# Hybrid NSA, pooling and HGRN2 block: four HGRN decay levels joined into two products of 192 queries, evictions moved from VectorE to ScalarE, and the compression slabs placed four later

## The chip, the cores and the metric

One core of a Trainium2 chip runs the kernel. The metric is the device time of one execution in microseconds (us). In what follows, PE is TensorE (matrix products), DVE is VectorE, ACT is ScalarE, POOL is GpSimd, and SP is the engine that issues the transfers.

## What is computed

One layer over 256 tokens of width 1024, in float32. The normalised input is multiplied by one wide matrix `w_in`, and the columns feed three mixers: sparse attention with compressed, selected and windowed keys, causal pooling, and HGRN2, a gated linear recurrence. Each mixer's output is gated, projected, merged and sent through `w_out`. The change lies in HGRN2, whose reference is, per chunk:

```
A = jnp.cumsum(lf, axis=2)
o_inter = jnp.einsum('bhtd,bhde->bhte', qq * jnp.exp(A), S)
rel = jnp.where(tri[:, :, None], A[:, :, :, None, :] - A[:, :, None, :, :], -jnp.inf)
att = jnp.einsum('bhtd,bhsd,bhtsd->bhts', qq, kk, jnp.exp(rel))
o_intra = jnp.einsum('bhts,bhse->bhte', att, vv)
```

`lf` is the logarithm of the forget gate. The score of query t and key s is a sum over 128 channels of q·k·exp(A[t] − A[s]). The exponent depends on both, and the kernel splits it at an edge e that lies between s and t: exp(A[t] − A[e]) goes into the query and exp(A[e] − A[s]) into the key, so that a plain matrix product gives the score and neither factor can overflow.

## The kernel before

**Slabs.** Every large product is cut into slabs of 256 output columns. `plan_slabs` lists 67 of them, numbered from 0, and every engine walks that list in order. Slabs 0 to 3 are the forget gates (`f`), 4 to 11 are HGRN queries and values in turn (`hq`, `hv`), 12 and 13 the keys and values of the compression (`kc`, `vc`), 14 and 15 attention values (`vs`, `vw`), 16 the attention gates (`gate`, 48 columns), 17 a query slab (`q`), 18 to 21 the pooling input (`bv`), and then the rest. A slab's weights land in `W` by a transfer. ACT rounds them to a high part `WH` (`hi`, L420), DVE subtracts that from `W` for a low part `WL` (`lo`, L603), and PE multiplies three pairs of parts into one PSUM bank: 48 matmuls at L970, 24 for `gate`. Two PSUM banks alternate, so `read(s)` on ACT or DVE must have emptied the bank of slab s before the product of slab s + 2 begins. `WL` has two buffers, so `lo(s)` waits for the end of product s − 2.

**HGRN between the slabs.** There are 8 heads of 256 tokens, and a unit u is one head's half of 128 tokens: 16 units, numbered 0 to 15. With `U0 = 9`, PE issues in slab 9 + u, ahead of that slab's product, `hg_scores(u)` and then `hg_values(u - 1)`. Before the change a unit's scores are five products of 64 queries (edges at multiples of 64, 32, 16, 8 and 4 tokens, L995), one of 128 queries for blocks of 4 tokens (L996) and, for the second half of a head, one across the halves (L999). Values are L1011 and L1013. At slabs 14, 18, 22 and 26 PE adds a sum of squares for the head norm (L1041).

What prepares a unit, in the order of the chain:

- DVE, at slabs 2, 6, 10 and 14: `scan` (L624), the running sum A of two heads (a pair).
- POOL: 12 subtractions for a pair (L348, L350, L352). Pairs 2 and 3 also wait until the scores of 4(p − 1) units are done, since the tiles are used again: pair 3 waits for unit 7, in slab 16.
- ACT, at slabs 6, 10, 14 and 18: exponentials of the pair (L433 to L439).
- DVE, at slab 7 + 2h: the multiplications of head h (L648 to L652), 14 instructions. `hg_scores` of the head waits for them (`s_hmul`).
- DVE, at slab s, `early(s)`: the masks of unit s − 9. It copies each product's valid part into `PM` (L708, L709, L716). Each is chained to the one before it. `hg_values(u)` waits for them (`s_hmask`).
- DVE, at slabs 11 + 2h, copies head h's result out of PSUM (L636), and ACT squares it (L443). At slabs 14, 18, 22 and 26 ACT turns the sums of squares into a factor with two table loads (L450, L451), and DVE multiplies two heads by it (`norm`, L639, waits `s_hrs`).

For slabs 9 to 24 the order of DVE within slab s is: `early(s)`, `lo(s + 1)`, the scan, norm and head multiplications that fall on s, and `read(s)`. The order of ACT is: exponentials, squares and norm factor of s, `read(s)`, `hi(s + 3)`. Every engine executes its list in order.

Of the kernel before, what the change touches and what calls it, by code (L numbers as in the profile page):

```python
# [26 lines left out]
LEVELS = (128, 64, 32, 16, 8, 4)  # L27
NLV = len(LEVELS)
SMALL_K, SMALL_Q = NLV, NLV + 1

# [7 lines left out]
K_MASK, K_ID, K_ONE = 0, 448, 576  # L38
K_BLOCK = K_MASK + 64 * (NLV - 1)
K_CMASK, K_VALID, K_COUNT = 704, 734, 736  # L40
K_ROWS, K_ALL = 800, 804
# [32 lines left out]
BY_ACT = ("f", "gate", "bv", "q", "ks", "kw", "silu", "merge", "out")  # L74
BY_DVE = ("hq", "hv", "kc", "vc", "ks", "kw", "vs", "vw", "q", "silu", "branch", "out")
# [13 lines left out]
def trunk(nc, x, small, consts, w_in, cmp_w, pool_w, w_branch, w_out, post_norm, out):  # L89
# [14 lines left out]
    with ctx:  # L104
# [42 lines left out]
        QK = [R[:, 4 + 2 * b:6 + 2 * b, :].rearrange("p a (l h t) -> p (a l) h t", h=2, t=T) for b in range(2)]  # L147
# [174 lines left out]
        def _(pool):  # L322
# [12 lines left out]
            for p in range(4):  # L335
# [7 lines left out]
                for i, b in enumerate(LEVELS):  # L343
                    n = 2 * T // (2 * b)
                    av = a2.rearrange("p (n w) -> p n w", w=2 * b)
                    dv = QK[p % 2][:, i].rearrange("p h t -> p (h t)").rearrange("p (n w) -> p n w", w=2 * b)
                    edge = av[:, :, b - 1:b].to_broadcast((P, n, b))
                    last = pool.tensor_tensor(dv[:, :, 0:b], edge, av[:, :, 0:b], ALU.subtract)  # L348
                    if i:
                        pool.tensor_tensor(dv[:, :, b:2 * b], av[:, :, b:2 * b], edge, ALU.subtract)  # L350
                mid = RHO[:, p].rearrange("p (n a) -> p n a", a=1).to_broadcast((P, 2 * T // 4, 4))
                pool.tensor_tensor(QK[p % 2][:, SMALL_K].rearrange("p h (n w) -> p (h n) w", w=4),  # L352
# [54 lines left out]
        def _(act):  # L407
# [14 lines left out]
            def mix(s):  # L422
# [5 lines left out]
                for p in range(4):  # L428
                    if s == U0 - 3 + 4 * p:
                        act.wait_ge(s_sub, p + 1)  # L430
                        act.wait_ge(s_scan, p + 1)
                        q = QK[p % 2]
                        act.activation(q[:, 0, :, P:T], HA[:, 2 * p:2 * p + 2, P:T], ACT.Exp)  # L433
                        act.activation(q[:, 0, :, 0:P], q[:, 0, :, 0:P], ACT.Exp)
                        act.activation(q[:, 1:NLV].rearrange("p l h t -> p (l h t)"),
                                       q[:, 1:NLV].rearrange("p l h t -> p (l h t)"), ACT.Exp)
                        small = q[:, SMALL_K].rearrange("p h t -> p (h t)")
                        act.activation(q[:, SMALL_Q].rearrange("p h t -> p (h t)"), small, ACT.Exp)
# [69 lines left out]
            def read(s):  # L508
# [4 lines left out]
                if kind == "f":  # L513
# [76 lines left out]
        def _(dve):  # L590
# [27 lines left out]
            def mix(s):  # L618
# [14 lines left out]
                for h in range(HG):  # L633
                    if s == U0 + 2 + 2 * h:
                        dve.wait_ge(s_hpv, 2 * h + 2)
                        dve.tensor_copy(OC[:, h, :], ps[:, 6, 0:T]).then_inc(s_hoc, 1)  # L636
                    if s == U0 + 5 + 4 * (h // 2):
                        dve.wait_ge(s_hrs, h // 2 + 1)
                        dve.scalar_tensor_tensor(out=OC[:, h, :], in0=OC[:, h, :], scalar=st_hn[:, h:h + 1], in1=RS[:, h % 2],  # L639
                                                 op0=ALU.mult, op1=ALU.mult).then_inc(s_hn, 1)  # L640
                for h in range(HG):
                    if s == U0 - 2 + 2 * h:
                        dve.wait_ge(s_hexp, h // 2 + 1)
                        for i, b in enumerate(LEVELS):
                            ev = QK[h // 2 % 2][:, i, h % 2].rearrange("p (n w) -> p n w", w=2 * b)
# [4 lines left out]
                        sk, sq_ = QK[h // 2 % 2][:, SMALL_K, h % 2], QK[h // 2 % 2][:, SMALL_Q, h % 2]  # L650
# [134 lines left out]
            def read(s):  # L785
# [458 lines left out]
```

## Time and profile before

| | |
|---|---|
| time, median of 3 runs | 491.25 us (491.23 to 491.64) |
| the profiled execution | 491.25 us, of which the span is 489.4 us |
| busy PE, DVE, ACT, POOL | 474.8, 359.8, 255.9, 157.4 us |
| PE clock granted | 0.999 of 2.4 GHz over the span |
| share of the chain that ended last | PE 88%, DVE 9% |

The span runs from the first to the last instruction. A busy time is a sum over an engine's instructions as the profiler models them. What an instruction costs in a dense row is the distance between the starts of two neighbours, which for PE is shorter than the printed duration, since matmuls overlap.

### The profile page before, as it was taken

The page shows a single profiled execution, that of the slowest core. Times are in us where ns is not written, and L with a number is a line of the kernel's source. Part 1 is how long each engine was busy: PE and PEld are TensorE (multiplying, and loading weights), DVE is VectorE, ACT ScalarE, POOL GpSimd, SP SyncE. Part 2 cuts the span into 40 slices and gives each one's busy share as a digit, 9 for nine tenths or more (in the row PEclk, how much of TensorE's full clock was granted, in tenths as well). Part 3 has the DMA queues.
Part 4 walks back from the last instruction along what each step waited for, and adds up shares of the span by engine and source line. Part 5 has one row for each costly group of instructions (what it writes and reads, how often), then busy time and mean ns, then how long its engine had stood idle before and what let it go on. Part 6 is the DMA issues. An engine that isn't in the chain of part 4 may idle for free.

```text
span 489.4 us, 9629 instructions
## 1 busy us (share of the span) xinstructions
PE 474.8 (97%) x3938; PEld 462.8 (95%) x3938; DVE 359.8 (74%) x647; ACT 255.9 (52%) x379; POOL 157.4 (32%) x157
## 2 busy tenths in 40 slices
PE   3999999999999999999999999999999999999995
PEld 3999999999899999999999999999999999999995
DVE  4897999899978775989696755888674357655653
ACT  6966635363484555844366444566554245433541
POOL 1072800702800006992067334546645220000000
PEclk9999999999999999999999999999999999999999
DMA  9965553325525485355537235234435535767502
GB/s 298 322 193 176 173 173 93 98 86 173 173 88 172 137 209 173 97 173 174 171 107 239 87 90 168 88 102 158 130 129 173 174 95 192 232 218 255 173 1 86
DMA packets 77030, 76.43 MB, mean 156 GB/s; under 512 B 6783, under 2 KB 75775, under 8 KB 76987
## 3 DMA queue, kind: packets, MB, share of 16 engines
q1 hardware_dynamic: 76699, 75.64, 49.5%
q8 instruction: 31, 0.51, 0.4%
q10 hardware_dynamic: 288, 0.18, 0.2%
q14 instruction: 12, 0.10, 0.1%
HBM read 74.77 MB, written 1.05 MB: 155 GB/s over the span
## 4 chain that ended last, share of the span: by engine, by line
PE 88%; DVE 9%; DMA 1%; issue 1%; ACT 0%; DVEq 0%
PE ps L970 71%; PE ps L1142 3%; DVE WL L603 3%; PE ps L995 2%; PE ps L1094 2%; PE ps L1083 1%; PE ps L1158 1%; DVE R L648 1%; DVE CP L813 1%; DVE R L649 1%; PE ps L1110 1%; DMA R<-x 1%; DVE PM L716 1%; PE ps L1097 1%; PE ps L1112 1%
## 5 line engine op out<-in xcount | busy, mean ns | idle before, releaser
L970 PE MATMUL ps<-hH,WL 128*128 128x256 f32 x696 | 200.6, 288 | 1.0 <-DVE WL L603 1.0
L970 PE MATMUL ps<-hL,WH 128*128 128x256 f32 x696 | 197.7, 284 | 0.0
L970 PE MATMUL ps<-hH,WH 128*128 128x256 f32 x696 | 197.7, 284 | 0.0
L603 DVE TENSOR_TENSOR WL<-W,WH 128x2048 fp32r<-128x2048 f32 x66 | 152.2, 2307 | 16.1 <-PE ps L970 15.7
L420 ACT ACTIVATE WH<-W 128x2048 fp32r<-128x2048 f32 x66 | 124.6, 1889 | 58.4 <-PE ps L970 58.3
L970 PEld LDWEIGHTS ps<-hH,WL 128*128 128x128 f32 x696 | 132.8, 191 | 2.2 <-DVE WL L603 1.2
L970 PEld LDWEIGHTS ps<-hL,WH 128*128 128x128 f32 x696 | 132.8, 191 | 0.8 <-issue 0.7
L970 PEld LDWEIGHTS ps<-hH,WH 128*128 128x128 f32 x696 | 132.8, 191 | 0.0
L381 POOL TENSOR_SCALAR R<-R,st 128x256 f32<-128x256 f32 x32 | 29.2, 923 | 80.1 <-DVE st L782 80.1
L970 PE MATMUL ps<-bH,WL 128*128 128x256 f32 x192 | 54.9, 286 | 0.0
L970 PE MATMUL ps<-bL,WH 128*128 128x256 f32 x192 | 54.3, 283 | 0.0
L970 PE MATMUL ps<-bH,WH 128*128 128x256 f32 x192 | 54.3, 283 | 0.0
L541 ACT ACTIVATE TG<-ps 128x512 f32<-128x512 f32 x24 | 14.4, 599 | 64.8 <-PE ps L970 64.8
L348 POOL TENSOR_TENSOR R<-R 128x256 f32<-128x256 f32 x24 | 24.1, 1011 | 74.5 <-PE ps L999 49.1
L970 PE MATMUL ps<-WL,hH 128*128 128x256 f32 x160 | 46.0, 287 | 0.9 <-DVE WL L603 0.9
L970 PE MATMUL ps<-WH,hL 128*128 128x256 f32 x160 | 45.3, 283 | 0.0
L970 PE MATMUL ps<-WH,hH 128*128 128x256 f32 x160 | 45.3, 283 | 0.0
L970 PEld LDWEIGHTS ps<-bH,WL 128*128 128x128 f32 x192 | 36.8, 192 | 0.2 <-issue 0.2
L970 PEld LDWEIGHTS ps<-bL,WH 128*128 128x128 f32 x192 | 36.8, 192 | 0.1
L970 PEld LDWEIGHTS ps<-bH,WH 128*128 128x128 f32 x192 | 36.8, 192 | 0.0
L384 POOL TENSOR_SCALAR R<-R,st 128x128 f32<-128x128 f32 x32 | 35.8, 1131 | 0.0
L970 PEld LDWEIGHTS ps<-WL,hH 128*128 128x128 f32 x160 | 30.7, 192 | 1.5 <-DVE WL L603 1.3
(191 smaller groups left out, 756.0 us busy)
## 6 DMA issues: line engine op xcount, KB each, us to landing
W<-w_in SPq DMA_DIRECT2D x49, 1024.0 KB, 5.2
W<-w_branch SPq DMA_DIRECT2D x12, 1024.0 KB, 5.0
W<-w_out SPq DMA_DIRECT2D x4, 1024.0 KB, 5.4
R<-x SPq DMA_DIRECT2D x2, 512.0 KB, 4.6
W<-w_in SPq DMA_DIRECT2D x2, 512.0 KB, 6.7
R<-cmp_w SPq DMA_DIRECT2D x2, 512.0 KB, 8.4
OC<-pool_w SPq DMA_DIRECT2D x4, 256.0 KB, 5.8
R<-x SPq DMA_DIRECT2D x1, 1024.0 KB, 7.2
```

The lines of the kernel that those rows point to most:

```text
L348: last = pool.tensor_tensor(dv[:, :, 0:b], edge, av[:, :, 0:b], ALU.subtract)
L381: pool.tensor_scalar(pp[:, 256 * j:256 * j + 256], pp[:, 256 * j:256 * j + 256], w[:, j:j + 1], None, ALU.mult)
L384: last = pool.tensor_scalar(pp[:, 512 + 128 * j:640 + 128 * j], pp[:, 512 + 128 * j:640 + 128 * j], w[:, 2 + j:3 + j], None, ALU.mult)
L420: act.activation(WH[:, s % 3, :, 0:n], W[:, s % 3, :, 0:n], ACT.Copy).then_inc(s_hi, 1)
L541: act.activation(TG[:, tslot(s), :], bank(s), ACT.Tanh, scale=0.5).then_inc(s_read_a, 1)
L603: dve.tensor_tensor(WL[:, s % 2, :, 0:n], W[:, s % 3, :, 0:n], WH[:, s % 3, :, 0:n], ALU.subtract).then_inc(s_lo, 1)
L648: dve.tensor_tensor(ev[:, :, 0:b], ev[:, :, 0:b], kv[:, :, 0:b], ALU.mult)
L649: dve.tensor_tensor(ev[:, :, b:2 * b], ev[:, :, b:2 * b], qv[:, :, b:2 * b], ALU.mult)
L970: mm = pe.matmul(o, l, r, start=(k == 0 and j == 0 and not (split and c)), stop=(k == KC - 1 and j == 2 and not (split and not c)))
L995: pe.matmul(ps[:, b0, 64 * (lv - 1):64 * lv], t, up, start=(lv == 1), stop=False)
L1094: pe.matmul(ps[:, 2, :], queries(h, 1), KS[:, part, g].rearrange("p a t -> p (a t)"), start=(part == 0), stop=(part == 1))
L1142: mm = pe.matmul(ps[64 * hh:64 * hh + 64, 6, at:T], v, p, start=(j == 0), stop=(j == count - 1))
```

## The change

The edges at 32 and 16 become one product, and so do those at 8 and 4 (`RADIX = (16, 4)`). For blocks of b tokens in groups of four, block j's queries are laid out once for every earlier block of their group: three blocks reach back one, two reach back two, one reaches back three (`STEPS`), six blocks of queries where there were four blocks of tokens. A key has one decay factor, to its own block's end (`OWN`), and the query copy carries the rest (`REACH`). The edges at 64 (`HALF`) and 128 (`TOP`) and the blocks of 4 tokens stay. `TOP` is now in another tile, `CVD`. ACT instead of DVE now reads `hq`, `hv`, `vs` and `vw` out of PSUM and copies the heads' results. `kc` and `vc` move from slabs 12 and 13 to 16 and 17, so that `vs`, `vw`, `gate` and `q` stand at 12 to 15.

```diff
-LEVELS = (128, 64, 32, 16, 8, 4)
-NLV = len(LEVELS)
-SMALL_K, SMALL_Q = NLV, NLV + 1
+RADIX = (16, 4)
+STEPS = ((0, 3, 1), (3, 2, 2), (5, 1, 3))
...
-    out += [("kc", 0, "in", C_KC), ("vc", 0, "in", C_VC), ("vs", 0, "in", C_VS), ("vw", 0, "in", C_VW),
-            ("gate", 0, "in", C_GATE), ("q", 2, "in", C_Q + 2 * SLAB)]
+    out += [("vs", 0, "in", C_VS), ("vw", 0, "in", C_VW), ("gate", 0, "in", C_GATE), ("q", 2, "in", C_Q + 2 * SLAB),
+            ("kc", 0, "in", C_KC), ("vc", 0, "in", C_VC)]
...
-BY_ACT = ("f", "gate", "bv", "q", "ks", "kw", "silu", "merge", "out")
-BY_DVE = ("hq", "hv", "kc", "vc", "ks", "kw", "vs", "vw", "q", "silu", "branch", "out")
+BY_ACT = ("f", "hq", "hv", "vs", "vw", "gate", "bv", "q", "ks", "kw", "silu", "merge", "out")
+BY_DVE = ("kc", "vc", "ks", "kw", "q", "silu", "branch", "out")
...
+        DEC = [R[:, 4 + 2 * b:6 + 2 * b, :].rearrange("p a n -> p (a n)") for b in range(2)]
+        TOP = [CVD[:, 2 * b:2 * b + 2, :] for b in range(2)]
+        HALF = [d[:, 0:512].rearrange("p (h t) -> p h t", h=2) for d in DEC]
+        OWN = [[d[:, 512 + 1280 * r:1024 + 1280 * r].rearrange("p (h t) -> p h t", h=2) for r in range(2)] for d in DEC]
+        REACH = [[d[:, 1024 + 1280 * r:1792 + 1280 * r].rearrange("p (h t) -> p h t", h=2) for r in range(2)]
+                 for d in DEC]
+        SMALL_K = [d[:, 3072:3584].rearrange("p (h t) -> p h t", h=2) for d in DEC]
+        SMALL_Q = [d[:, 3584:4096].rearrange("p (h t) -> p h t", h=2) for d in DEC]
...
+                for r, b in enumerate(RADIX):
+                    n = 2 * T // b
+                    av = a2.rearrange("p (n w) -> p n w", w=b)
+                    pool.tensor_tensor(OWN[p % 2][r].rearrange("p h (n w) -> p (h n) w", w=b),
+                                       av[:, :, b - 1:b].to_broadcast((P, n, b)), av, ALU.subtract)
+                    aw = a2.rearrange("p (n j w) -> p n j w", j=4, w=b)
+                    to = REACH[p % 2][r].rearrange("p h (n j w) -> p (h n) j w", j=6, w=b)
+                    for at, count, far in STEPS:
+                        pool.tensor_tensor(to[:, :, at:at + count], aw[:, :, far:4],
+                                           aw[:, :, 0:count, b - 1:b].to_broadcast((P, n // 4, count, b)), ALU.subtract)
                 mid = RHO[:, p].rearrange("p (n a) -> p n a", a=1).to_broadcast((P, 2 * T // 4, 4))
...
-                        act.wait_ge(s_hoc, h + 1)
-                        act.activation(SQ[:, h % 2], OC[:, h, :], ACT.Square).then_inc(s_hsq, 1)
+                        act.wait_ge(s_hpv, 2 * h + 2)
+                        act.wait_ge(s_scan, h // 2 + 1)
+                        act.activation(SQ[:, h % 2], ps[:, 6, 0:T], ACT.Square).then_inc(s_hsq, 1)
+                        act.activation(OC[:, h, :], ps[:, 6, 0:T], ACT.Copy).then_inc(s_hoc, 1)
...
+                if kind == "hq":
+                    act.activation(HQ[:, 2 * n:2 * n + 2, :], b2, ACT.Copy).then_inc(s_read_a, 1)
+                elif kind == "hv":
+                    act.activation(HV[:, :, SLAB * n:SLAB * n + SLAB], b2, ACT.Copy).then_inc(s_read_a, 1)
+                elif kind in ("vs", "vw"):
+                    act.activation(VV[:, 0 if kind == "vs" else 1], b2, ACT.Copy).then_inc(s_read_a, 1)
...
-                    if s == U0 + 2 + 2 * h:
-                        dve.wait_ge(s_hpv, 2 * h + 2)
-                        dve.tensor_copy(OC[:, h, :], ps[:, 6, 0:T]).then_inc(s_hoc, 1)
                     if s == U0 + 5 + 4 * (h // 2):
                         dve.wait_ge(s_hrs, h // 2 + 1)
+                        dve.wait_ge(s_hoc, h + 1)
...
+                        for r, b in enumerate(RADIX):
+                            dve.tensor_tensor(OWN[e][r][:, hp], OWN[e][r][:, hp], HK[:, h], ALU.mult)
+                            qv = HQ[:, h].rearrange("p (n j w) -> p n j w", j=4, w=b)
+                            ev = REACH[e][r][:, hp].rearrange("p (n j w) -> p n j w", j=6, w=b)
+                            for at, count, far in STEPS:
+                                dve.tensor_tensor(ev[:, :, at:at + count], ev[:, :, at:at + count], qv[:, :, far:4],
+                                                  ALU.mult)
...
-                    for lv in range(1, NLV):
-                        b = LEVELS[lv]
-                        r = slice(0, b if lv == 1 else P)
-                        to = PM[r, u % 2, 0:P].rearrange("p (n w) -> p n w", w=2 * b)[:, :, b:2 * b]
-                        c = slice(64 * (lv - 1), 64 * lv)
-                        last = dve.copy_predicated(to, K[r, c].bitcast(mybir.dt.uint32).rearrange(
-                            "p (n w) -> p n w", w=b), ps[r, b0, c].rearrange("p (n w) -> p n w", w=b))
-                        if lv < NLV - 1:
-                            link(last)
-                    last.then_inc(s_hmask, 1)
+                                             ps[:, b0 + 1, P:2 * P]))
+                    for r, b in enumerate(RADIX):
+                        c = slice(192 * r, 192 * r + 192)
+                        to = PM[:, u % 2, 0:P].rearrange("p (n j w) -> p n j w", j=4, w=b)
+                        on = K[:, c].bitcast(mybir.dt.uint32).rearrange("p (n j w) -> p n j w", j=6, w=b)
+                        src = ps[:, b0, c].rearrange("p (n j w) -> p n j w", j=6, w=b)
+                        for at, count, far in STEPS:
+                            link(dve.copy_predicated(to[:, :, far:4], on[:, :, at:at + count], src[:, :, at:at + count]))
+                    dve.tensor_copy(PM[0:64, u % 2, 64:P], ps[0:64, b0, 384:448]).then_inc(s_hmask, 1)
                 h = s - H0 - 2
...
-                q = QK[p % 2]
-                for lv in range(1, NLV):
-                    b = LEVELS[lv]
-                    t = q[:, lv, hp, P * i:P * i + P]
-                    up = t.rearrange("p (n w) -> p n w", w=2 * b)[:, :, b:2 * b]
-                    pe.matmul(ps[:, b0, 64 * (lv - 1):64 * lv], t, up, start=(lv == 1), stop=False)
-                mm = pe.matmul(ps[:, b0, K_BLOCK:K_BLOCK + P], q[:, SMALL_K, hp, P * i:P * i + P],
-                               q[:, SMALL_Q, hp, P * i:P * i + P], start=False, stop=True)
+                e, t = p % 2, slice(P * i, P * i + P)
+                for r in range(2):
+                    pe.matmul(ps[:, b0, 192 * r:192 * r + 192], OWN[e][r][:, hp, t],
+                              REACH[e][r][:, hp, 192 * i:192 * i + 192], start=(r == 0), stop=False)
+                pe.matmul(ps[:, b0, 384:448], HALF[e][:, hp, t], HALF[e][:, hp, P * i + 64:P * i + P],
+                          start=False, stop=True)
+                mm = pe.matmul(ps[:, b0 + 1, P:2 * P], SMALL_K[e][:, hp, t], SMALL_Q[e][:, hp, t],
+                               start=True, stop=(i == 0))
                 if i:
-                    mm = pe.matmul(ps[:, b0 + 1, 0:P], q[:, 0, hp, 0:P], q[:, 0, hp, P:T], start=True, stop=True)
+                    mm = pe.matmul(ps[:, b0 + 1, 0:P], TOP[e][:, hp, 0:P], TOP[e][:, hp, P:T], start=False, stop=True)
                 mm.then_inc(s_hp, 1)
```

**PE, the scores of an odd unit and the values of the one before it.** In the rows below `R` holds the decayed keys and queries and `K`-named operands are constants. Before:

```order
L995 MATMUL ps<-R 128x64 x5
L996 MATMUL ps<-R 128x128
L999 MATMUL ps<-R 128x128
L1011 MATMUL ps<-PM,R 128x128
```

After the change:

```order
L1013 MATMUL ps<-R 128x192 x2
L1015 MATMUL ps<-R 128x64
L1017 MATMUL ps<-R 128x128
L1020 MATMUL ps<-CVD 128x128
L1032 MATMUL ps<-PM,R 128x128
```

Five products of 64 queries become two of 192 and one of 64. What follows them stays.

**ACT, slabs 13 and 14.** Before, from the square of head 1 (L443) to the next `hi`. `WH<-W 128x8x48` is the narrow `gate` slab, L433 to L439 the exponentials of pair 2, L450 and L451 the norm factor of pair 0:

```order
L443 ACTIVATE TG<-OC 128x256
L420 ACTIVATE WH<-W 128x8x48
L433 ACTIVATE R<-R 128x2x128
L434 ACTIVATE R<-R 128x2x128
L435 ACTIVATE R<-R 128x2560
L438 ACTIVATE R<-R 128x512
L439 ACTIVATE R<-R 128x512
L450 ACT_TABLE_LOAD
L450 ACTIVATE TG<-ps,st 128x512
L451 ACT_TABLE_LOAD
L451 ACTIVATE TG<-TG 128x512
L420 ACTIVATE WH<-W 128x2048
```

After the change, from the copy of head 1's result:

```order
L458 ACTIVATE OC<-ps 128x256
L534 ACTIVATE VV<-ps 128x512
L435 ACTIVATE WH<-W 128x2048
L448 ACTIVATE CVD<-R 128x2x128
L449 ACTIVATE CVD<-CVD 128x2x128
L450 ACTIVATE R<-R 128x3072
L451 ACTIVATE R<-R 128x512
L452 ACTIVATE R<-R 128x512
L465 ACT_TABLE_LOAD
L465 ACTIVATE TG<-ps,st 128x512
L466 ACT_TABLE_LOAD
L466 ACTIVATE TG<-TG 128x512
```

The read of `vw` (L534) stands ahead of a full `hi` where a narrow one stood, and the largest exponential is 3072 wide.

**DVE, slab 15.** Before, from the narrow `lo` of slab 16 (L603): the copy of head 2, and the first six of the 14 multiplications of head 4:

```order
L603 TENSOR_TENSOR WL<-W,WH 128x8x48
L636 COPY OC<-ps 128x256
L648 TENSOR_TENSOR R<-R 128x128
L649 TENSOR_TENSOR R<-R 128x128
L648 TENSOR_TENSOR R<-R 128x2x64
L649 TENSOR_TENSOR R<-R 128x2x64
L648 TENSOR_TENSOR R<-R 128x4x32
L649 TENSOR_TENSOR R<-R 128x4x32
```

After the change, from the end of the multiplications of head 4, after which the `q` slab is read, to the read of `kc` (L836) in slab 16:

```order
L673 TENSOR_TENSOR R<-R 128x256
L677 TENSOR_TENSOR R<-R 128x16x12
L677 TENSOR_TENSOR R<-R 128x16x8
L677 TENSOR_TENSOR R<-R 128x16x4
L680 TENSOR_TENSOR R<-R 128x256
L681 TENSOR_TENSOR R<-R 128x256
L823 TENSOR_TENSOR QS<-ps,QS 64x2x256 x2
L737 COPY PM<-ps 128x128
L738 COPY_PREDICATED PM<-K,ps 128x128
```

The head's multiplications by tokens in pairs of halves become, for each radix, one over 256 keys and three over 192 queries' worth in steps of 12, 8 and 4 (or 48, 32 and 16) columns. They still number 14. The mask stage that follows has six chained copies of 96, 64 and 32 columns, twice, and a plain one of 64 instead of five of 64. The narrow `lo` moves from slab 15 to slab 13, since it belongs to `gate`.

## Rows read from the trace of the kernel before

**Rows 1.** Page: busy time of PE, and the chain that ended last.

```profile
PE 474.8 (97%) x3938; PEld 462.8 (95%) x3938; DVE 359.8 (74%) x647; ACT 255.9 (52%) x379; POOL 157.4 (32%) x157
...
PE 88%; DVE 9%; DMA 1%; issue 1%; ACT 0%; DVEq 0%
```

**Rows 2.** Waits of PE: total us, times, longest us.

```profile
PE ps L1166 <- DVE R L869: 7.4, 1, 7.4
PE ps L970 <- DVE WL L603: 1.9, 3, 1.0
```

**Rows 3.** Chain in order of time: start us, us until the next piece, what.

```profile
78.86 1.06 PE ps L995 x10
79.93 0.28 PE ps L996 x2
80.65 5.75 PE ps L970 x48
...
125.47 6.02 PE ps L970 x48
...
133.28 0.86 PE ps L1041 x2
...
268.40 1.73 PE ps L1083 x8
```

**Rows 4.** Timeline of DVE, slabs 12, 13 and 17: start us, us, instruction, shape, count.

```profile
97.36 0.30 DVE L709 COPY_PREDICATED PM<-K,ps 128x128 f32<-128x128 uint32 x1
97.69 1.27 DVE L716 COPY_PREDICATED PM<-K,ps 64x64 f32<-64x64 uint32 x5
98.87 2.29 DVE L603 TENSOR_TENSOR WL<-W,WH 128x2048 fp32r<-128x2048 f32 x1
...
101.41 0.28 DVE L648 TENSOR_TENSOR R<-R 128x128 f32<-128x128 f32 x1
...
103.83 0.43 DVE L651 TENSOR_TENSOR R<-R 128x256 f32<-128x256 f32 x1
...
104.49 3.34 DVE L813 TENSOR_TENSOR CP<-ps,V 64x240 f32<-64x240 f32 x8
...
134.67 1.39 DVE L798 TENSOR_TENSOR QS<-ps,QS 64x512 fp32r<-64x512 f32 x2
```

**Rows 5.** Timeline of DVE, slab 7, head 0.

```profile
56.04 0.70 DVE L648 TENSOR_TENSOR R<-R 128x128 f32<-128x128 f32 x1
56.66 0.73 DVE L649 TENSOR_TENSOR R<-R 128x128 f32<-128x128 f32 x1
```

**Rows 6.** Timeline of POOL, pair 1 beside rows 5, and pair 2.

```profile
56.55 0.69 POOL L350 TENSOR_TENSOR R<-R 128x256 f32<-128x256 f32 x1
...
89.84 2.66 POOL L348 TENSOR_TENSOR R<-R 128x256 f32<-128x256 f32 x1
...
93.05 0.61 POOL L348 TENSOR_TENSOR R<-R 128x256 f32<-128x256 f32 x1
...
96.68 1.11 POOL L352 TENSOR_TENSOR R<-R,BR 128x512 f32<-128x512 f32 x1
```

**Rows 7.** Timeline of ACT, slab 14, and a read of slab 18.

```profile
102.26 0.40 ACT L433 ACTIVATE R<-R 128x256 f32<-128x256 f32 x1
...
110.09 1.90 ACT L420 ACTIVATE WH<-W 128x2048 fp32r<-128x2048 f32 x1
...
142.40 0.58 ACT L520 ACTIVATE R<-ps 128x512 f32<-128x512 f32 x1
```

**Rows 8.** Timelines of DVE and POOL where pair 3 starts beside head 4.

```profile
120.06 0.42 DVE L652 TENSOR_TENSOR R<-R 128x256 f32<-128x256 f32 x1
...
119.75 1.77 POOL L348 TENSOR_TENSOR R<-R 128x256 f32<-128x256 f32 x2 [21.97 <-PE ps L999]
```

**Rows 9.** Windows after the last matmul: busy us of the engines (count), PEclk, DMA share, GB/s.

```profile
484.00:485.00 1.00, 0.17 (x2) 0.00 (x0) 0.46 (x3) 0.57 (x3) 0.00 (x0) 1.00 0.62 229
488.00:489.00 1.00, 0.00 (x0) 0.00 (x0) 0.00 (x0) 0.00 (x0) 0.00 (x0) 0.53 0.50 188
```

More of the change, by code:

```diff
@@ L35 @@
 GATES = 3 * HEADS
[L38 to L41, printed above, removed]
+K_MASK, K_BLOCK, K_ID, K_ONE = 0, 384, 512, 640
+K_CMASK, K_VALID, K_COUNT = 768, 798, 800
+K_ROWS, K_ALL = 864, 868
 K_CAUSAL = K_ALL
@@ L146, in trunk @@
         HV = R[:, 3, :].rearrange("p (i n) -> p i n", i=TT)
-        QK = [R[:, 4 + 2 * b:6 + 2 * b, :].rearrange("p a (l h t) -> p (a l) h t", h=2, t=T) for b in range(2)]
+        DEC = [R[:, 4 + 2 * b:6 + 2 * b, :].rearrange("p a n -> p (a n)") for b in range(2)]
[6 more added lines that the diff above has]
+        SMALL_Q = [d[:, 3584:4096].rearrange("p (h t) -> p h t", h=2) for d in DEC]
         xin = R[:, 4, :].rearrange("p (i n) -> p i n", i=TT)
@@ L431, in mix @@
                         act.wait_ge(s_scan, p + 1)
-                        q = QK[p % 2]
[L433 to L438, printed above, removed]
+                        top, small = TOP[p % 2], SMALL_K[p % 2].rearrange("p h t -> p (h t)")
+                        act.activation(top[:, :, P:T], HA[:, 2 * p:2 * p + 2, P:T], ACT.Exp)
+                        act.activation(top[:, :, 0:P], top[:, :, 0:P], ACT.Exp)
+                        act.activation(DEC[p % 2][:, 0:3072], DEC[p % 2][:, 0:3072], ACT.Exp)
+                        act.activation(SMALL_Q[p % 2].rearrange("p h t -> p (h t)"), small, ACT.Exp)
                         act.activation(small, small, ACT.Exp, scale=-1.0).then_inc(s_hexp, 1)
@@ L643, in mix @@
                         dve.wait_ge(s_hexp, h // 2 + 1)
-                        for i, b in enumerate(LEVELS):
-                            ev = QK[h // 2 % 2][:, i, h % 2].rearrange("p (n w) -> p n w", w=2 * b)
+                        dve.wait_ge(s_read_a, ACT_READS[WHERE[("hq", h // 2)]])
+                        e, hp = h // 2 % 2, h % 2
+                        for b, to in ((128, TOP), (64, HALF)):
+                            ev = to[e][:, hp].rearrange("p (n w) -> p n w", w=2 * b)
                             kv = HK[:, h].rearrange("p (n w) -> p n w", w=2 * b)
@@ L793, in read @@
                 b2 = b.rearrange("p (c t) -> p c t", c=2)
-                if kind == "hq":
-                    last = dve.tensor_copy(HQ[:, 2 * n:2 * n + 2, :], b2)
-                elif kind == "q":
+                if kind == "q":
                     for src, own, other in query_halves(s):
                         last = dve.tensor_tensor(other, src, own, ALU.subtract)
-                elif kind == "hv":
-                    last = dve.tensor_copy(HV[:, :, SLAB * n:SLAB * n + SLAB], b2)
                 elif kind in ("kc", "vc"):
@@ L818, in read @@
                         last = dve.tensor_tensor(other, src, hi_own, ALU.subtract)
-                elif kind in ("vs", "vw"):
-                    last = dve.tensor_copy(VV[:, 0 if kind == "vs" else 1], b2)
                 elif kind == "silu":
@@ L1004, in hg_values @@
                 pe.wait_ge(s_hmask, u + 1)
-                pe.wait_ge(s_read_v, DVE_READS[WHERE[("hv", h // 2)]])
+                pe.wait_ge(s_read_a, ACT_READS[WHERE[("hv", h // 2)]])
                 if h and i == 0:
@@ L1120, in at_values @@
                 if pair == 0:
+                    pe.wait_ge(s_read_a, ACT_READS[WHERE[("vw", 0)]])
                     pe.wait_ge(s_pct, 1)
@@ L1189, in constant_table @@
     s = np.arange(P)[:, None]
-    j = np.arange(64)[None, :]
-    for n, b in enumerate(LEVELS[1:]):
-        t = (j // b) * 2 * b + b + j % b
-        k[:, K_MASK + 64 * n:K_MASK + 64 * n + 64] = (s // (2 * b) == t // (2 * b)) & (s % (2 * b) < b)
+    j = np.arange(192)
+    for n, b in enumerate(RADIX):
+        step = j // b % 6
+        far = np.array([1, 1, 1, 2, 2, 3])[step]
+        key = 4 * (j // (6 * b)) + np.array([0, 1, 2, 0, 1, 0])[step]
+        assert (far + key % 4 < 4).all()
+        k[:, K_MASK + 192 * n:K_MASK + 192 * n + 192] = s // b == key[None, :]
     t = np.arange(P)[None, :]
```

17 lines of the change are left out of this document (8 added, 9 removed).

## Prediction, made before the changed kernel had run

> **What bounds the kernel now.** I read the busy times first: PE works in 97% of the span and is 88% of the chain that ended last [rows 1]. The table of waits then shows how little is left to win by removing waits: after its start PE idles three times, 1.9 us in all, each time for `lo` on DVE [rows 2]. The chain in order of time shows the beat of an HGRN slab: 1.79 us of scores and values (from 78.86 to 80.65), then 5.75 us of product, 7.54 us together [rows 3]. So a shorter score block is a gain only while DVE keeps up. The 9% of DVE in the chain is the warning: where `kc` and `vc` add 3.34 us each [rows 4], DVE has more work than a slab of 7.54 us has room for. I therefore went through the DVE timeline slab by slab, and through POOL's beside it.
>
> **PE.** Each float32 product is two passes. Ten passes over 64 queries take 1.06 us, 0.106 each; eight over 256 take 1.73 us, 0.216 each [rows 3]. The narrow ones stand on a floor, the wide ones cost 0.84 ns a column, so a pass over 192 should take 0.162. Eight passes (0.85) become four (0.65): 0.20 us less per unit, 3.2 us over 16 units. Bounds: four passes at the floor of 0.106 save 6.8 us in all; four at the 256-wide 0.216 save nothing. A score block is now 1.59 us; the scores of an even unit end 1.14 us into it, those of an odd one 1.36.
>
> **DVE per slab.** Masks: one of 128 columns takes 0.33 to the next start (97.36 to 97.69), and five of 64 take 1.18 to `lo` at 98.87, the last of them unchained [rows 4]. Six chained ones of 96, 64 and 32 columns average about 0.25, and the plain copy 0.2: 0.33 + 1.50 + 0.20 = 2.03 in place of 1.51, with bounds of 1.8 and 2.3. Multiplications of a head: twelve of 128 columns take 2.42 (101.41 to 103.83), 0.20 each, and those of 256 take 0.33 each (103.83 to 104.49) [rows 4]. By that slope 192 and 64 cost 0.27 and 0.13, so a head takes 4 × 0.20 + 2 × (0.33 + 0.27 + 0.20 + 0.13) + 2 × 0.33 = 3.3 in place of 3.1. Copies of `hq`, `hv`, `vs`, `vw` and the results leave DVE. On ACT each read is at most 0.58 [rows 7], and ACT is busy in 52% of the span [rows 1] with a single 1.9 us `hi` in most slabs [rows 7], so outside slab 14 they cost nothing; if that cover went, a slab would pay 0.6. No transfer changes.
>
> **POOL.** Alone it takes 0.58 for 256 columns (93.05 to the next start) and 1.11 for 512 [rows 6]; 384 and 128 lie at 0.85 and 0.32. A pair is 3 × 0.58 + 2 × (1.11 + 0.85 + 0.58 + 0.32) + 1.11 = 8.6 us, against 7.5. What matters more: when POOL and a DVE instruction with two SBUF inputs meet, one waits. At 56 us DVE's 0.20 became 0.62 (56.04 to 56.66), in step with POOL's 0.66 [rows 5, 6], and one POOL subtraction took 2.66 across a `lo` [rows 6]. The Trainium skill, "SBUF — State Buffer", SBUF: two separate sides, states it as an exclusive lock held for a whole instruction; by that rule the trace agrees, and without it the collision below would cost nothing.
>
> **The walk.** First, slab 14, with T the end of product 13. `gate` now stands here, with half a product. PE: block 1.59, squares 0.86 [rows 3], half a product 2.9, block 1.59, product 5.75, block 1.59: it wants product 16 at T + 14.3. ACT must do the read of `vw` 0.5, a full `hi` 1.8, then what took 102.26 to 110.09, 7.8, and 0.4 for 512 more columns [rows 7]: the norm factor is there at T + 10.5. DVE waits for it and does norm (two of 256, 0.8), the masks of unit 6 (2.03) and `lo(16)` (2.2 [rows 4]): T + 15.6. PE waits 1.3. Before, DVE came to the norm so late that this factor was ready.
>
> Second, slab 15, from X = T + 15.6, when product 16 starts (6.0 after a stall [rows 3]). DVE begins head 4. POOL's pair 3 has been free since the scores of unit 7, at T + 14.05, and was held by `lo(16)`; it starts at X too. They alternate, one DVE instruction for each of POOL's twelve, so head 4 lasts as long as the pair: 8.6, with 0.1 of each DVE instruction between, 9.8, and the last two multiplications, 10.4 us instead of 3.3. Behind it on DVE stand `q` 1.4 [rows 4], the masks of unit 7 with their plain copy 2.2, and `lo(17)` 2.2: X + 16.3. PE wanted product 17 at 6.0 + 1.6 = X + 7.6. It waits 8.7, of which 4.4 for the multiplications (`s_hmul`) ahead of unit 8's scores, 2.5 for the masks, 1.8 for `lo`.
>
> Third, `kc` and `vc`, from Y, the start of product 17. DVE: `kc` 3.4, masks 2.0, `lo` 2.2, head 5 3.3, `vc` 3.4, masks 2.2, `lo(19)` 2.2: Y + 18.7. PE: 6.0, block 1.59 with 0.86, 5.75, block 1.59: Y + 15.8. It waits 3.0. After that DVE has one head or none per slab and catches up; later slabs stand as before.
>
> Slab 9 has head 0 against pair 1, which grows by 1.1 us while DVE loses two reads ahead of it; I take 1.1 us for its wait of 0.5.
>
> Sum: waits 1.1 + 1.3 + 8.7 + 3.0 = 14.1 in place of 1.9; 0.25 for one more restart (6.02 against 5.75 [rows 3]); 3.2 saved. 491.25 + 14.1 − 1.9 + 0.25 − 3.2 = 500.5. The profiled execution took 491.25, the median too. The same walk through the old order gives product 17 some 2 us too late, because it lets POOL in at 119.75 where head 4 in fact ran on to 120.4 and POOL waited (1.77 for two) [rows 8]. I take 1 us off: **499.5**.
>
> **The rivals.** *The collision does not happen* (POOL is not yet asking, or yields as at 119.75). Then head 4 takes 3.3, the slab 15 wait is 9.1 − 7.6 = 1.5, and the waits sum to 0.5 + 1.3 + 1.5 + 3.0 = 6.3: 492.7. For it speaks only the one place where POOL was starting cold; here it has waited since T + 14.05.
>
> *Faster:* the reads taken from DVE let it reach head 4 before unit 7's scores release POOL, and `kc` and `vc` fall where it has slack. Then PE keeps 3.2 and loses only 0.5: 491.25 − 3.2 − 1.9 + 0.5 = 486.6. It decides at slab 14: head 4 must end by T + 14.05, so start by T + 10.7, which is 4.9 us earlier than in my walk. The wait for the norm is 2.8 of these; that and 2 us of masks and `lo` would have to go. Against it: the ACT chain is rows of before, moved by a full `hi`.
>
> *The clock falls.* The last matmul lies in the window from 484 us; the granted clock is 1.00 until 488 and 0.53 on average in the next window [rows 9]. So PE at rest for about 4 us went to 1.2 GHz, and the wait of 4.4 us in slab 17 is as long. Half a product at half speed would add 2.9: 502.4. The Trainium skill, "TensorE: Matmul & The Clock Gate", What's actually happening, says that an idle engine falls to the lower level and comes back after sustained work; by that rule, the trace agrees for the fall, and no row shows a fall in mid-kernel.
>
> *No change* needs gains and waits to cancel, between the second rival and the first.
>
> **How the numbers follow.** My case 0.58, with 495 to 503 as its own range (masks at 1.8 or 2.3 move three mask stages and with them 1.5 us, POOL's 4-dimensional subtractions at 10% more or less 1.5 us, the bounds of the passes 3 us either way in part, since a shorter PE stage only waits longer). Clock 0.10, no collision 0.14, faster 0.13, no change 0.05. The first three hold 0.82, so the range is 492 to 504. This kernel can be told from no change beyond 0.2%. Faster 0.14, same 0.05, slower 0.81.
>
> **What would show it.** Right: 192-wide products at 0.16 a pass; DVE idle before the norm in slab 14; head 4's multiplications at 0.6 to 1.1 each beside POOL; PE idle for L681's multiplications before unit 8 and for `lo` in slabs 16, 17 and 19. Wrong: head 4 over before POOL starts pair 3, which takes away 7 us; or masks dearer or cheaper than 2.03.

## The result, and the profile after

The changed kernel takes 494.93 us (493.23 to 496.15, 6 runs) against 491.31 us before: a ratio of 1.0066, with a 95% interval of 1.0047 to 1.0086. It is slower by 3.6 us. The forecast was 499.5 us: the sign was right, the size was more than twice too large, and the way there tells why.

The page of the changed kernel's profile first, with the rows that answer to [rows 1], and the row of the granted clock, where each digit is a fortieth of the span:

```profile
span 493.2 us, 9557 instructions
...
PE 473.5 (96%) x3874; PEld 461.3 (94%) x3874; DVE 363.4 (74%) x661; ACT 264.0 (54%) x397; POOL 162.5 (33%) x157
...
PEclk9999999999989999999999999999999999999998
...
PE 85%; DVE 9%; ACT 4%; issue 2%; DMA 1%; DVEq 0%; ACTq 0%
```

PE has less to do than before and takes a smaller part of the chain. ACT, which had 0%, has 4%. The clock row has a dent in the twelfth slice, about 136 to 148 us. The waits of PE answer to [rows 2]; columns as there:

```profile
PE ps L991 <- DVE WL L625: 5.6, 4, 1.7
PE ps L1032 <- DVE PM L747: 1.5, 1, 1.5
```

PE waits 7.1 us for DVE after its start in place of 1.9: 0.84 in slab 9, 1.71 before product 16, 1.58 before product 17, and 1.45 and 1.49 in slab 19. From 101.0 us the chain that ended last stands on ACT, up to the norm factor at 111.2, and from there on DVE up to 144.8. The chain in order of time, for [rows 3]:

```profile
78.59 0.65 PE ps L1013 x4
79.41 0.28 PE ps L1017 x2
80.14 5.76 PE ps L991 x48
...
144.87 7.50 PE ps L991 x48
...
153.91 5.76 PE ps L991 x48
```

Four passes over 192 queries take 0.65 us, as worked out. The whole block, from 78.59 to 80.14, is 1.55 us in place of 1.79, a little better than the 1.59 that I had, and saves 3.8 us over 16 units. The product at 144.87 takes 7.50 us where one after a wait takes 6.02 [rows 3]. The windows around it (busy us of PE, PEld, DVE, ACT, POOL with counts, then the granted clock) show the reason:

```profile
136.00:140.00 4.00, 4.00 (x36) 4.00 (x35) 3.90 (x12) 3.97 (x5) 0.00 (x0) 1.00 0.53 187
140.00:144.00 4.00, 1.93 (x13) 1.55 (x12) 3.71 (x11) 3.97 (x5) 0.00 (x0) 1.00 0.01 2
144.00:146.00 2.00, 1.13 (x7) 1.14 (x8) 1.97 (x5) 1.07 (x3) 0.00 (x0) 0.84 0.09 8
146.00:148.00 2.00, 2.00 (x11) 2.00 (x11) 1.79 (x8) 0.00 (x0) 0.00 (x0) 0.50 0.93 278
148.00:150.00 2.00, 2.00 (x16) 2.00 (x15) 2.00 (x3) 0.00 (x0) 0.00 (x0) 0.81 0.67 238
```

Between 140 and 144 us PE was busy 1.93 of 4 us; most of the rest lies in the two waits of 1.45 and 1.49 us. Then the clock was granted at 0.50, 1.2 GHz, and came back before 150 us. This cost 1.5 us (7.50 against 6.02). The Trainium skill, "TensorE: Matmul & The Clock Gate", What's actually happening, says that the clock is set by how busy the engine has been recently; by that rule, the trace agrees.

The place that matters most is slab 15. DVE's timeline, to be held against [rows 4]:

```profile
111.21 0.88 DVE L659 SCALAR_TENSOR_TENSOR OC<-OC,st,TG 128x256 f32<-128x256 f32 x2 [3.12 <-ACT TG L466]
...
114.07 2.27 DVE L625 TENSOR_TENSOR WL<-W,WH 128x2048 fp32r<-128x2048 f32 x1
116.27 0.28 DVE L670 TENSOR_TENSOR CVD<-CVD,R 128x128 f32<-128x128 f32 x1
...
119.29 0.41 DVE L681 TENSOR_TENSOR R<-R 128x256 f32<-128x256 f32 x1
```

POOL's, to be held against [rows 8]:

```profile
114.47 5.71 POOL L353 TENSOR_TENSOR CVD<-R 128x256 f32<-128x256 f32 x1 [16.09 <-PE ps L1020]
120.14 0.61 POOL L353 TENSOR_TENSOR R<-R 128x256 f32<-128x256 f32 x1
```

DVE waits 3.12 us for the norm factor, where 2.8 had been forecast. But the 14 multiplications of head 4 follow each other undisturbed, from 116.27 to 119.7 us. It is POOL's first subtraction of pair 3 that waits, 5.71 us, through the rest of `lo(16)` and the whole head. My walk had it the other way round.

### The profile page after: what moved, and what is told of

Its sections match the earlier page's. It is cut to its first block, busy times and chain, and to the rows that moved or that the text cites. A ratio compares the mean times of both kernels' runs of the same rounds, so it can differ in the third digit from the quotient of the medians.

```text
span 493.2 us, 9557 instructions
## 1 busy us (share of the span) xinstructions
PE 473.5 (96%) x3874; PEld 461.3 (94%) x3874; DVE 363.4 (74%) x661; ACT 264.0 (54%) x397; POOL 162.5 (33%) x157
## 4 chain that ended last, share of the span: by engine, by line
PE 85%; DVE 9%; ACT 4%; issue 2%; DMA 1%; DVEq 0%; ACTq 0%
PE ps L991 69%; PE ps L1164 3%; DVE WL L625 2%; PE ps L1115 2%; PE ps L1104 1%; PE ps L1180 1%; PE ps L1013 1%; DVE PM L746 1%; DVE CP L836 1%; DVE R L677 1%; PE ps L1131 1%; ACT R L450 1%; ACT WH L435 1%; DMA R<-x 1%; PE ps L1118 1%
## 5 line engine op out<-in xcount | busy, mean ns | idle before, releaser
L399 POOL TENSOR_SCALAR R<-R,st 128x128 f32<-128x128 f32 x32 | 34.3, 1085 | 0.0
L382 POOL TENSOR_TENSOR R<-R 128x510 f32<-128x510 f32 (+3 forms) x10 | 13.4, 1342 | 60.8 <-PE ps L1034 60.1
```

The source lines that it names most:

```text
L382: link(pool.tensor_tensor(dst[:, :, sh:T], cur[:, :, sh:T], cur[:, :, 0:T - sh], ALU.add))
L399: last = pool.tensor_scalar(pp[:, 512 + 128 * j:640 + 128 * j], pp[:, 512 + 128 * j:640 + 128 * j], w[:, 2 + j:3 + j], None, ALU.mult)
```

## The experiments

Two things had to be settled: which part of the change costs the time, and which of DVE and POOL goes first where both want to read SBUF. Times are medians of 4 or more runs beside the kernel before on the same chip (491.2 to 491.4 us).

**Only the evictions.** The kernel before, with these lines of the change alone (with the waits that follow from them):

```diff
-BY_ACT = ("f", "gate", "bv", "q", "ks", "kw", "silu", "merge", "out")
-BY_DVE = ("hq", "hv", "kc", "vc", "ks", "kw", "vs", "vw", "q", "silu", "branch", "out")
+BY_ACT = ("f", "hq", "hv", "vs", "vw", "gate", "bv", "q", "ks", "kw", "silu", "merge", "out")
+BY_DVE = ("kc", "vc", "ks", "kw", "q", "silu", "branch", "out")
...
-                        act.activation(SQ[:, h % 2], OC[:, h, :], ACT.Square).then_inc(s_hsq, 1)
+                        act.activation(SQ[:, h % 2], ps[:, 6, 0:T], ACT.Square).then_inc(s_hsq, 1)
+                        act.activation(OC[:, h, :], ps[:, 6, 0:T], ACT.Copy).then_inc(s_hoc, 1)
```

> The kernel before, with the reads of hq, hv, vs, vw and of the heads' results on ScalarE and nothing else changed: same levels, same order of slabs. Theory A (VectorE is what the waits hang on, and its masks and multiplications of the joined levels eat more than the reads free): all waits of TensorE except the one at the start go, 1.9 us less, so about 489.3 us. Rival B (the reads on ScalarE delay the high parts or the norm factor, and this is where the change lost): 491.3 us or more.

Measured: 488.98 us, ratio 0.9952 (0.9939 to 0.9964). The table of waits of PE for this kernel has one line, the start:

```profile
PE ps L1169 <- DVE R L871: 7.5, 1, 7.5
```

All waits on DVE behind the start are gone, as theory A has it, and the reads on ACT cost nothing that PE sees.

**Only the joined products.** The changed kernel with `BY_ACT`, `BY_DVE`, the result copies and the slab order as before:

```diff
-BY_ACT = ("f", "hq", "hv", "vs", "vw", "gate", "bv", "q", "ks", "kw", "silu", "merge", "out")
-BY_DVE = ("kc", "vc", "ks", "kw", "q", "silu", "branch", "out")
+BY_ACT = ("f", "gate", "bv", "q", "ks", "kw", "silu", "merge", "out")
+BY_DVE = ("hq", "hv", "kc", "vc", "ks", "kw", "vs", "vw", "q", "silu", "branch", "out")
```

> The kernel before with the two joined products alone: VectorE keeps its reads and the slabs keep their order. TensorE's scores and values take 1.55 us a unit in place of 1.79, 3.8 us less in all. Theory A (per unit VectorE pays 0.55 us more for masks and 0.25 us per head for multiplications, and it was already short of time in slabs 9 to 15): waits of TensorE of 10 to 14 us, time 496 to 500 us. Rival B (VectorE has slack outside the compression slabs and the saving survives): 489 to 491 us.

Measured: 495.8 us, ratio 1.0090 (1.0076 to 1.0104). The sign is theory A's; the size falls just short of its lower end. PE's waits after the start, eight in all:

```profile
PE ps L989 <- DVE WL L616: 5.0, 5, 1.5
PE ps L1030 <- DVE PM L739: 0.7, 1, 0.7
PE ps L1030 <- DVE OC L649: 0.6, 1, 0.6
PE ps L1011 <- DVE R L673: 0.3, 1, 0.3
```

They sum to 6.6 us, not 10 to 14. Waits of 4.7 us more against 3.8 us saved make only 0.9 of the 4.5 us. The clock makes another 1.5: it fell behind waits of 0.67 and 1.49 us, and from the start of the product behind them to the next scores 7.36 us pass (114.84 to 122.20), where 5.86 do at the full clock (125.47 to 131.33 in the kernel before). The windows there, columns as above:

```profile
114.00:116.00 2.00, 1.16 (x5) 1.17 (x6) 2.00 (x5) 0.41 (x1) 0.00 (x0) 0.72 0.07 12
116.00:118.00 2.00, 2.00 (x12) 2.00 (x11) 1.97 (x6) 0.00 (x0) 0.00 (x0) 0.50 1.02 325
```

Restarts can hold up to 1.3 us more, 0.27 for each of five more waits; this is an estimate from the 6.02 against 5.75 us of [rows 3]. The last 0.8 us are not assigned. So the joined products, by themselves, lose: the waits for DVE, with the slower clock and the restarts behind them, take more than PE saves.

**The change with the old slab order.**

```diff
-    out += [("vs", 0, "in", C_VS), ("vw", 0, "in", C_VW), ("gate", 0, "in", C_GATE), ("q", 2, "in", C_Q + 2 * SLAB),
-            ("kc", 0, "in", C_KC), ("vc", 0, "in", C_VC)]
+    out += [("kc", 0, "in", C_KC), ("vc", 0, "in", C_VC), ("vs", 0, "in", C_VS), ("vw", 0, "in", C_VW),
+            ("gate", 0, "in", C_GATE), ("q", 2, "in", C_Q + 2 * SLAB)]
```

> The changed kernel with kc and vc back in slabs 12 and 13. Theory A (the order of the slabs costs time, because gate's half product then stands in slab 14, where ScalarE has the norm factor to make and VectorE waits 3.1 us for it): product 14 is whole again, the wait of VectorE before the norm falls under 1 us, the waits of TensorE fall from 7.1 to about 4 to 5 us in slabs 15 to 19, and the time is about 492 us, 2 to 3 us less than with the change. Rival B (the two slabs cost the same 3.3 us of VectorE each wherever they stand): the waits move to slabs 14 to 17 and the time stays within 1 us of 494.9.

Measured: 490.71 us, ratio 0.9990 (0.9981 to 0.9998). Moving the slabs is thus what turned a kernel that was level with before into a slower one: it costs 4.2 us (494.9 against 490.7), more than the whole difference of 3.6. Theory A had expected 2 to 3 us. It left out the clock, which does not fall here and had cost 1.5. PE's waits sum to 4.8 us here (4.5 for `lo`, 0.3 for a mask), and the norm multiplications stand in the timeline without any idle time before them:

```profile
108.61 0.63 ACT L466 ACTIVATE TG<-TG 128x512 f32<-128x512 f32 x1
113.72 0.88 DVE L659 SCALAR_TENSOR_TENSOR OC<-OC,st,TG 128x256 f32<-128x256 f32 x2
```

This edit does not separate the short `gate` slab from the place of `kc` and `vc`. ACT has the factor ready 1.9 us earlier than in the changed kernel (109.2 against 111.2), but DVE also comes to it 5.6 us later (113.7 against 108.1, the end of its scan), since both reads stand ahead of it. By these times the second difference alone would have removed the wait.

**The norm one slab later.**

```diff
-                    if s == U0 + 5 + 4 * (h // 2):
+                    if s == U0 + 6 + 4 * (h // 2):
                         dve.wait_ge(s_hrs, h // 2 + 1)
```

> The changed kernel with VectorE's norm multiplications one slab later (slabs 15, 19, 23, 27), which gives ScalarE a slab more for the factor. Theory A (the wait for the norm factor in slab 14 is on the path): VectorE no longer idles 3.1 us there, TensorE's wait of 1.7 us before product 16 goes and the one before product 17 falls to about 1 us, the time is about 492 us. Rival B (the backlog is made by kc and vc alone): the time saved is under 1 us, since later waits grow by what this one loses.

Measured: 491.81 us, ratio 1.0004 (0.9995 to 1.0013), 3.1 us less than the change. The wait before product 16 is gone and the one before product 17 is 0.89 us in place of 1.58. The two of slab 19 stand: 1.5 for the mask, 1.49 of the 3.2 for `lo`:

```profile
PE ps L991 <- DVE WL L625: 3.2, 3, 1.5
PE ps L1032 <- DVE PM L747: 1.5, 1, 1.5
```

**vc in slab 20, alone and with the late norm.** `kc` stays in slab 16, and three `bv` slabs come between it and `vc`:

```diff
-            ("kc", 0, "in", C_KC), ("vc", 0, "in", C_VC)]
+            ("kc", 0, "in", C_KC)]
     out += [("bv", n, "in", C_BV + n * SLAB) for n in range(4)]
+    out.insert(20, ("vc", 0, "in", C_VC))
```

> The changed kernel with vc in slab 20 instead of 17 and nothing else. Theory A (the two waits of slab 19 come from kc and vc in a row, the two of slabs 16 and 17 from the norm factor): the first two stay at 1.7 and 1.6 us, the last two go and the clock stays up, about 490 us. Rival B (the slabs' places hardly matter): 493.5 us or more.

Measured: 490.25 us, ratio 0.9980 (0.9971 to 0.9988). The waits are 0.84 (slab 9), 1.71 and 1.58:

```profile
PE ps L992 <- DVE WL L626: 4.1, 3, 1.7
```

> The changed kernel with the norm multiplications one slab later and vc in slab 20 instead of 17 (kc stays in 16). Theory A (TensorE waits where two compression reads stand in a row): of the waits only those before products 9 and 17 stay, 1.7 us in all; with the 2.95 us at slab 19, the lower clock behind it (1.5 us) and a restart or two gone, the time is about 487 us, below both kernels. Rival B (the backlog is there without vc): a wait of 1 us or more stays in slabs 18 to 22, the time is 489 us or more.

Measured: 486.86 us, ratio 0.9911 (0.9898 to 0.9923). This version beats the kernel before by 4.4 us and the evictions alone by 2.1 us. Its table of PE's waits has one line for DVE after the start:

```profile
PE ps L992 <- DVE WL L626: 1.7, 2, 0.9
```

The clock row of its page has no dent:

```profile
PEclk9999999999999999999999999999999999999999
```

Both kernels came out where theory A put them. The joined products pay once DVE has room: in the kernel with the evictions alone no wait was left to remove, so the 2.1 us come from the shorter blocks (3.8 saved, 1.7 of waits).

**A gap ahead of head 4.** One memset into an unused tile on DVE, between `lo(16)` and the multiplications of head 4:

```diff
                     if s == U0 - 2 + 2 * h:
+                        if h == 4:
+                            dve.memset(PT1[:, 0:256], 0.0)
                         dve.wait_ge(s_hexp, h // 2 + 1)
```

> The changed kernel with one memset of 256 columns of an unused tile on VectorE right before the multiplications of head 4, behind lo(16). It reads nothing. Theory A (VectorE keeps the SBUF port from GpSimd for as long as its two-input instructions stand back to back, and loses it at the first gap; then they alternate): GpSimd's first subtraction of pair 3 ends about 0.6 us after lo(16), head 4's multiplications take about 10 us instead of 3.4, TensorE waits 7 us more in slab 17, time 501 us or more. Rival B (VectorE is served first whenever it asks): the memset costs its own 0.3 us, head 4 stays under 4.5 us, time within 1.5 us of 494.9.

Measured: 500.02 us, ratio 1.0177 (1.0164 to 1.0191), 5.1 us above the change for an instruction of 0.27 us. DVE, and then POOL, in the timeline of this kernel:

```profile
116.59 0.27 DVE L664 MEMSET PT<- 128x256 f32 x1
116.79 0.42 DVE L672 TENSOR_TENSOR CVD<-CVD,R 128x128 f32<-128x128 f32 x1
117.14 0.70 DVE L673 TENSOR_TENSOR CVD<-CVD,R 128x128 f32<-128x128 f32 x1
...
126.22 0.41 DVE L683 TENSOR_TENSOR R<-R 128x256 f32<-128x256 f32 x1
```

```profile
114.72 2.34 POOL L353 TENSOR_TENSOR CVD<-R 128x256 f32<-128x256 f32 x1 [16.10 <-PE ps L1022]
117.03 0.66 POOL L353 TENSOR_TENSOR R<-R 128x256 f32<-128x256 f32 x1
```

POOL's first subtraction gets in during the memset and ends at 117.06. From then on each multiplication waits for one subtraction, and head 4 lasts from 116.79 to 126.6, 9.8 us in place of 3.4. This is the collision of the prediction, started by a gap that the changed kernel doesn't have. PE waits 4.0 us for the multiplications (I had 4.4) and 6.4 before product 17 in all (I had 8.7), 4.8 more than in the changed kernel and not theory A's 7. Its clock fell during the 4.0 us, as the rival of the prediction had it, and stands at 0.50 from 126 to 135 us. So had the collision come, the 499.5 would have been met partly by luck: its waits of 8.7 and 3.0 us (6.4 and 1.5 here) were too long, and it left out the clock.

**Controls: the gap behind head 4, and in its middle.** The same memset after the head's last multiplication:

> The same memset behind the multiplications of head 4, as a control. Both theories: head 4 takes 3.4 us as in the changed kernel, GpSimd starts behind it, time within 1 us of 494.9.

Measured: 495.25 us, ratio 1.0075 (1.0060 to 1.0089). POOL's first subtraction takes 5.71 us again. Then the memset after the fourth of the fourteen:

> The changed kernel with the memset of VectorE behind the fourth of head 4's 14 multiplications instead of ahead of the first. Theory A (any gap lets GpSimd in, and from then on they alternate): four multiplications at 0.2 us, GpSimd's first subtraction ends some 0.6 us behind them, the other ten at GpSimd's pace of 0.6 to 1.1 us, so head 4 takes 8 to 9.5 us and TensorE waits 5 to 6 us more in slab 17: 499 to 501 us. Rival B (only the place right behind lo(16) matters): time within 1 us of 494.9.

Measured: 498.80 us, ratio 1.0151 (1.0136 to 1.0165), just under theory A's 499. Four multiplications pass at 0.2 us each, then the rest at POOL's pace; the head ends at 125.7, 9.0 us after its start. PE waits 5.4 us before product 17, 3.8 more than in the changed kernel.

**GpSimd not at rest.** What remained was slab 7, where POOL was let in right behind a `lo` with no gap on DVE [rows 5, 6]. There POOL was in the middle of its pair. The first try puts a memset on POOL ahead of pair 3:

```diff
+                if p == 3:
+                    pool.memset(PT1[:, 0:256], 0.0)
                 for b, to in ((128, TOP), (64, HALF)):
```

> The changed kernel with one memset of 256 columns of an unused tile on GpSimd, right before the first subtraction of pair 3, so that this subtraction is not GpSimd's first instruction after a rest. Theory C (GpSimd's first instruction after a rest loses to a run of VectorE's, a following one is let in at the first boundary, as in slab 7 of both kernels): if the memset itself gets through, the subtraction is let in right behind lo(16), head 4 takes about 10 us, the time is 500 us. Theory A (what decides is only whether VectorE's run has a gap): GpSimd's subtraction starts behind head 4, the time is within 1 us of 494.9; then slab 7 needs another explanation.

Measured: 495.34 us, ratio 1.0081 (1.0068 to 1.0094). The subtraction behind the memset takes 5.45 us. Theory C falls, as far as a memset, which reads nothing, ends a rest. The second try keeps POOL busy with reading instructions until `lo(16)` begins:

```diff
+                if p == 3:
+                    pool.wait_ge(s_hn, 2)
+                    pool.tensor_tensor(PT1[:, 0:768], K[:, 0:768], K[:, 0:768], ALU.subtract)
+                    pool.tensor_tensor(BR[:, 1, :], K[:, 0:512], K[:, 0:512], ALU.subtract)
                 if p >= 2:
                     pool.wait_ge(s_hp, 4 * (p - 1))
```

> The changed kernel with two subtractions on GpSimd ahead of pair 3, of 768 and 512 columns of the constants, into unused tiles, started by the norm multiplications of slab 14 (their results are used by nothing). They keep GpSimd's two-input run going from 112.3 us into the start of lo(16), as a pair's own subtractions do in slab 7. Theory D (who is let in is settled by the order of asking: a GpSimd instruction that already asks when VectorE's run begins is let in at the first boundary, one that comes in the middle of an instruction of the run is not let in before a gap): lo(16) starts up to 0.8 us late, pair 3 is let in right behind it, head 4's multiplications take about 9 us in place of 3.4, the time is about 500 us. Theory A (only a gap in VectorE's run counts): head 4 takes 3.4 us, the time is 495 to 496 us.

Measured: 500.53 us, ratio 1.0187 (1.0173 to 1.0201). DVE and then POOL:

```profile
114.34 2.76 DVE L629 TENSOR_TENSOR WL<-W,WH 128x2048 fp32r<-128x2048 f32 x1
117.02 0.70 DVE L674 TENSOR_TENSOR CVD<-CVD,R 128x128 f32<-128x128 f32 x1
```

```profile
113.91 1.04 POOL L345 TENSOR_TENSOR BR<-K 128x512 f32<-128x512 f32 x1
114.91 2.66 POOL L357 TENSOR_TENSOR CVD<-R 128x256 f32<-128x256 f32 x1
117.53 0.66 POOL L357 TENSOR_TENSOR R<-R 128x256 f32<-128x256 f32 x1
```

`lo(16)` first waits half a microsecond for POOL (2.76 in place of 2.27). POOL's next subtraction asks at 114.91, at once behind its predecessor and so as `lo(16)` takes over, and it is let in exactly at the boundary behind `lo(16)`: it ends at 117.57, and the first multiplication has to wait for it. Theory D's forecast holds here. What differs from the changed kernel is how POOL came: in a handover from a run of its own, or alone and 0.4 us into DVE's instruction (114.47 against 114.07). These are two things in one: the moment of asking, and whether POOL already is in a run of reading instructions. A place further on in the changed kernel speaks for the second. DVE, and then POOL:

```profile
201.29 3.04 DVE L625 TENSOR_TENSOR WL<-W,WH 128x2048 fp32r<-128x2048 f32 x1
204.25 1.65 DVE L659 SCALAR_TENSOR_TENSOR OC<-OC,st,TG 128x256 f32<-128x256 f32 x2
```

```profile
200.89 1.29 POOL L389 TENSOR_TENSOR R<-R 128x512 f32<-128x512 f32 x1
202.26 2.96 POOL L382 TENSOR_TENSOR R<-R 128x510 f32<-128x510 f32 x1
```

A `lo` of 2.27 us that ends at 204.33 began at about 202.06 (an estimate from its usual length), so POOL's addition at 202.26, behind a run of POOL's own, asked some 0.2 us into it. Nonetheless it was let in at the first boundary: the two norm multiplications behind that `lo` take 1.65 us in place of 0.88. So an instruction that comes in the middle can be let in without a gap, against the second half of theory D, and the order of asking is not shown to be what decides.

## Why the prediction was right in sign and wrong in size

**PE's saving** was forecast at 0.20 us a unit and measured 0.24, since the two passes over 64 queries behind the wide ones take 0.17 us together, where I had 0.21. This term was 0.6 us too small.

**DVE per slab.** The masks were forecast at 2.03 us and take 2.07 (79.73 to the next `lo` at 81.80); a head was forecast at 3.3 and takes 3.4. Both bounds were wider than needed.

**The walk, first stop.** PE's wait before product 16 was forecast at 1.3 and is 1.7. The late norm took it away together with DVE's 3.12 us of idle time, so that idle time is its cause. The prediction put it down to the short `gate` slab, which makes PE want product 16 early. The old order takes the idle time away, but it moves `kc` and `vc` as well, so the share of the short slab is not shown.

**The walk, second stop,** is the step that failed: "POOL's pair 3 has been free since the scores of unit 7 [...] and was held by `lo(16)`; it starts at X too. They alternate". POOL didn't start at X. It waited behind the whole head, and PE waited 1.58 us before product 17 instead of 8.7. This single term is 7.1 us of the sum. I had a row that spoke against it, POOL waiting at 119.75 [rows 8], and took it for an effect of a cold start worth 1 us, where POOL waits for the whole run here. The rival that was right is "The collision does not happen", at 492.7 us, with a chance of 0.14. Its waits of 6.3 us were 7.1 in fact.

**The walk, third stop.** Forecast 3.0 us for `kc` and `vc` in a row, measured 1.45 and 1.49. Moving `vc` to slab 20 took both away.

**Slab 9** was forecast at 1.1 and is 0.84.

**The clock.** I had it only as a rival, behind a wait of 4.4 us that didn't come. It fell all the same, behind two waits of 1.5 us in slab 19, and cost 1.5 us. The sum had nothing for it.

From the second rival's 492.7, 0.8 us of waits more, 1.5 us of clock and 0.6 us less for PE give 494.4, and the measured median is 494.9. The 0.5 us left are not assigned; each wait also makes the next product up to 0.27 us longer [rows 3].

**Which part costs what,** from the medians: the evictions bring 2.3 us (491.3 to 489.0). The joined products on top cost 1.7 (490.7). The new place of the slabs costs another 4.2 (494.9). Without the evictions the joined products cost 4.5. So this cost has no fixed size: it depends on how much room DVE has. The two cures do add: the late norm brings 3.1 us and the place of `vc` 4.7, and both together bring 8.1, since each clears waits of its own. Of the 4.7 us some 1.5 are the clock.

## What to carry to other kernels

A shorter TensorE block is worth its time only if the engine that feeds it has room: here 3.8 us saved were paid for with VectorE's masks, and came back only once two waits had been cleared. Before work is moved to another slab, walk every engine through the slabs around it: here VectorE lost the two long reads that had kept it busy until ScalarE was ready, idled 3.1 us, and met the same reads later, where they made TensorE wait. And where VectorE and GpSimd both work from SBUF, look for gaps in front of VectorE's run and in it, since one instruction of 0.27 us there changed the time by 4 to 5 us.

## What the runs showed of the hardware

Instructions of VectorE with two SBUF inputs that stand back to back kept a GpSimd subtraction waiting that arrived in the middle of the first, over 15 instructions and 5.71 us. A memset of VectorE ahead of the fourteen or among them let it in. After that the two alternated, instruction by instruction, and fourteen multiplications went from 3.4 to 9.8 us. A GpSimd subtraction that asked as VectorE's run began was let in at the first boundary (2.66 us across a `lo`), as in slab 7 of the kernel before. The Trainium skill, "SBUF — State Buffer", Who interferes with whom, says that issue order and not the kind of operation decides who blocks. The case at the first boundary agrees with it. The case without a gap does not: POOL asked 1.8 us before the first of the fourteen multiplications began (114.47 against 116.27) and came after all of them. What decides at a boundary stays open, between the moment of asking and whether GpSimd is already in a run of reading instructions; so does how it works inside.

The granted clock fell to 0.50 after two waits of 1.45 and 1.49 us with 0.7 us of work between them, not only after one long rest. It did so behind this pair of waits in all four profiled kernels that have it. Behind waits of 0.35 and 1.49 us (the old order) it stayed up. A single wait of 1.71 us before product 16 was followed by a fall in two kernels (the gap behind head 4 and the memset on POOL, with 7.3 us from the start of product 16 to the next scores, where 5.9 pass in the changed kernel) and by none in four others, so the length of the wait alone does not settle it.
